# Four block quads for three in each feed-forward chunk, two of their weight sums taken from a DRAM scratch

## The reference

```
h = rms_norm(x, g_mix);   x = x + hybrid_mixer(h, ..., w_in, ..., w_out)
h = rms_norm(x, g_xattn); x = x + memory_cross_attention(h, rms_norm(mem, g_mem), w_xq, w_xkv, w_xo)
h = rms_norm(x, g_ffn)
x = x + (silu(h @ w_gate) * (h @ w_up)) @ w_down
return rms_norm(x, g_final)
```

## Time and profile before

| | |
|---|---|
| median of 3 runs | 1197.07 us (1196.96 to 1198.46) |
| the profiled execution | 1196.37 us, span 1194.8 us |
| TensorE clock granted | 0.998 |
| busy: PE, DVE, ACT, POOL | 99%, 78%, 56%, 7% |
| moved by DMA | 234.52 MB, 196 GB/s over the span |

### The profile page before, as it was taken

One profiled execution on the slowest core, in us unless ns is written; L12 is line 12 of the kernel. 1 busy time (PEld: TensorE's weight loads), 2 busy tenths in 40 slices (PEclk: granted clock), 3 DMA queues, 4 the chain that ended last, 5 costly groups with the idle time before them and its releaser, 6 DMA issues.

```text
span 1194.8 us, 16408 instructions
## 1 busy us (share of the span) xinstructions
PE 1184.5 (99%) x5418; PEld 983.0 (82%) x5418; DVE 934.2 (78%) x1176; ACT 674.8 (56%) x883; POOL 83.6 (7%) x89
## 2 busy tenths in 40 slices
PE   9999999999999999999999999999999999999997
PEld 8888888888888888888888888888888888888885
DVE  6655555557855666999899899989989889988886
ACT  5665554546644575765556555655555555555553
POOL 0042332200210000000000000000000000000000
PEclk9999999999999999999999999999999999999999
DMA  9865455556455544466566566566656656665663
GB/s 344 293 211 176 161 173 180 171 175 227 163 191 183 189 159 141 160 211 190 198 201 203 176 209 226 166 203 197 211 184 202 209 210 203 211 222 175 203 205 141
DMA packets 65851, 234.52 MB, mean 196 GB/s; under 512 B 7696, under 2 KB 8464, under 8 KB 65424
## 3 DMA queue, kind: packets, MB, share of 16 engines
q1 hardware_dynamic: 63072, 225.60, 57.2%
q10 hardware_dynamic: 2736, 8.35, 1.9%
HBM read 231.83 MB, written 2.10 MB: 196 GB/s over the span
## 4 chain that ended last, share of the span: by engine, by line
PE 90%; DVE 6%; DMA 2%; ACT 1%; issue 1%; POOLq 0%; POOL 0%; ACTq 0%; SPq 0%; DVEq 0%
PE ps L489 23%; PE ps L491 23%; PE ps L490 23%; PE ps L732 6%; PE ps L733 6%; PE ps L734 6%; DVE wlo L1624 3%; DMA raw<-w_stream 2%; PE ps L521 1%; DVE wsum L1631 1%; DVE raw L1619 0%; DVE raw L1627 0%; ACT whi L1145 0%; DMA par<-params 0%; PE ps L604 0%
## 5 line engine op out<-in xcount | busy, mean ns | idle before, releaser
L1145 ACT ACTIVATE whi<-raw 128x1024 fp32r<-128x1024 f32 (+1 forms) x310 | 303.9, 991 | 212.5 <-DMA raw<-w_stream 95.7
L1624 DVE TENSOR_TENSOR wlo<-raw,whi 128x1024 fp32r<-128x1024 f32 (+1 forms) x310 | 346.4, 1138 | 19.4 <-ACT whi L1145 18.8
L1270 DVE TENSOR_TENSOR wlo<-raw,whi 128x1024 fp32r<-128x1024 f32 x160 | 198.5, 1245 | 111.4 <-ACT whi L893 111.2
L489 PE MATMUL ps<-whi,ahi 128*128 128x512 f32 x600 | 235.9, 393 | 0.0
L491 PE MATMUL ps<-whi,alo 128*128 128x512 f32 x600 | 234.0, 390 | 0.0
L490 PE MATMUL ps<-wlo,ahi 128*128 128x512 f32 x600 | 233.7, 390 | 0.0
L893 ACT ACTIVATE whi<-raw 128x1024 fp32r<-128x1024 f32 x160 | 168.4, 1058 | 107.0 <-PE ps L491 96.3
L489 PE MATMUL ps<-whi,bhi 128*128 128x512 f32 x448 | 180.2, 402 | 0.5 <-DVE blo L1363 0.5
L491 PE MATMUL ps<-whi,blo 128*128 128x512 f32 x448 | 175.3, 391 | 0.0
L490 PE MATMUL ps<-wlo,bhi 128*128 128x512 f32 x448 | 174.7, 390 | 0.0
L491 PEld LDWEIGHTS ps<-whi,alo 128*128 128x128 f32 x600 | 112.7, 188 | 23.5
(11 more groups left out here) (244 smaller groups left out, 1498.9 us busy)
## 6 DMA issues: line engine op xcount, KB each, us to landing
raw<-w_stream SPq DMA_DIRECT2D x422, 512.0 KB, 4.2
res<-x_in ACTq DMA_DIRECT2D x4, 512.0 KB, 7.7
stage<-mem_in ACTq DMA_DIRECT2D x4, 512.0 KB, 6.5
proj<-mem_T ACTq DMA_DIRECT2D x2, 1024.0 KB, 7.7
stage<-x_T SPq DMA_DIRECT2D x7, 256.0 KB, 6.8
y_out<-res SPq DMA_DIRECT2D x4, 320.0 KB, 3.1
raw<-w_stream SPq DMA_DIRECT2D x4, 256.0 KB, 4.8
gfin<-g_final ACTq DMA_DIRECT2D x1, 1024.0 KB, 4.9
```

The source lines that it names most:

```text
L489: nc.tensor.matmul(bank, lhsT=a_h, rhs=w_h, start=start, stop=False)
L1145: nc.scalar.activation(whi_here, src, ACT.Copy).then_inc(hi_ready, 1)
L1270: vec.tensor_tensor(tile_pair(wlo, j), tile_pair(raw, j), tile_pair(whi, j).bitcast(f32), ALU.subtract).then_inc(lo_ready, 1)
L1624: vec.tensor_tensor(lo_here, src, hi_here.bitcast(f32), ALU.subtract).then_inc(lo_ready, 1)
```

## The change

1. **Quads.** `QUADS` goes from 3 to 4, at places 2, 7, 12 and 17 of a chunk that now has 24 places. One ordinary step stands between two quads; the others stand at 0, 1 and 21 to 23. Chunk 0 thus has two ordinary steps ahead of its first quad, not three, and the first is of K pair 4, not 3. A chunk has 8 ordinary steps, not 10. The parts have 6, 3, 6 and 6 matmuls.
2. **Weights of a quad.** The signs of the form are changed so that the sums are T = [B11 + B12, B22 + B12] and two more of 512 columns. The first tile of a quad is Z = [B11, B22] (512 KB), the second only B21 (H, 256 KB), and T (512 KB) is a third load, from the DRAM scratch `tsums`. DVE per quad: low parts of 1024, 512, 1024 and 1024 columns, and two sums of 512 (`wsum`). Before: low parts of 512, 1024, 1024 and 1024, and sums of 512, 512 and 1024. ACT per quad: 1024, 512, 1024 and 1024 columns; before: 512 and three times 1024.
3. **The scratch.** There are 44 T tiles. For each, SP copies Z to `tsums` (512 KB, DRAM to DRAM), one copy after every four loads from step 12 on, and the last 7 one after each of chunks 0 to 6. POOL then issues an accumulating transfer that adds B12 to both halves (`add_weights`); each waits for its copy and for the accumulation before it. They stand between POOL's other work: one before the head loop, two per head, one every third step from the convolution on, four between the last two roots, then a loop.
4. **Where T lies.** Chunk 0's T tiles go to free SBUF; from chunk 1 on they take the place of `res`. In chunk 0, after the seventh weight load, SP writes `res` (2 MB) to `res_kept`; in the down projection it loads it back in four pieces of 512 KB, at places 4, 8, 12 and 16 of `DOWN`, and `down_combine` waits for all four.
5. **Small ones.** `s_forms`, `s_lows` and the casts between them cover four quads; ACT makes two more copies of activations (`araw`); `P1_AT`, `COMBINED`, `SILU_AT` go from 17, 18, 21 to 19, 21, 23.

```diff
-QUADS = 3
+QUADS = 4
-QUAD_AT = (3, 9, 14)
+QUAD_AT = (2, 7, 12, 17)
-GATE_STEPS = {0: 3, 1: 4, 2: 5, 7: 6, 8: 7}
-UP_STEPS = {13: 3, 18: 4, 19: 5, 20: 6, 21: 7}
+GATE_STEPS = {0: 4, 1: 5, 6: 6, 11: 7}
+UP_STEPS = {16: 4, 21: 5, 22: 6, 23: 7}
+RAW_TILES = ("D0", "D1", "Z0", "H0", "D2", "Z1", "H1", "D3", "Z2", "H2", "D4", "Z3", "H3", "D5", "D6", "D7")
+T_LOAD_AT = {0: 0, 4: 1, 7: 2, 10: 3}
+RES_SAVE_AT, RES_BACK_AT = 6, (4, 8, 12, 16)
...
+                    if n in T_LOAD_AT:
+                        m = T_LOAD_AT[n]
+                        if m == 0:
+                            sp.wait_ge(t_summed, ci * (16 * QUADS) + 16 * QUADS * (c + 1))
+                        sp.dma_start(t_tile(c, m), tsums[ci * QUADS + (c * QUADS + m)]).then_inc(t_loaded[m], 16)
...
+                    if c == 0 and n == RES_SAVE_AT:
+                        await_out(sp, G_FF - 1)
+                        sp.dma_start(res_kept, res[:]).then_inc(res_saved, 16)
...
+                sp.dma_start(tsums[i - COPY_FROM], stream[i + (J_Z - COPY_FROM)]).then_inc(t_copied, 16)
...
+            def add_weights(m, first=False):
+
+                pool.wait_ge(t_copied, m * 16 + 16)
+                if not first:
+                    pool.wait_ge(t_summed, m * 16)
+                both = tsums[m].rearrange("p (h n) -> p h n", h=2)
+                b12 = stream[m + J_W][:, GC:KS * GC].unsqueeze(1).to_broadcast([P, 2, GC])
+                nc.gpsimd.dma_start(both, b12, accum_op=ALU.add).then_inc(t_summed, 16)
...
+                if part == 1:
+                    b22, b21 = tile_pair(raw, j)[:, GC:KS * GC], tile_pair(raw, j + 1)[:, 0:GC]
+                    dve.wait_ge(t_loaded[q % QUADS], ci * 16 + 16 * (q // QUADS + 1))
...
+                    vec.tensor_tensor(wsum[:, 0:GC], t_tile(q // QUADS, q % QUADS)[:, 0:GC], b22,
+                                      ALU.add).then_inc(w_sums, 1)
+                    dve.wait_ge(w_sums, ci * (2 * QUADS) + (2 * q + 1))
+                    vec.tensor_tensor(wsum[:, GC:KS * GC], wsum[:, 0:GC], b21, ALU.add).then_inc(w_sums, 1)
```

More of the change, by code:

```diff
@@ L464, in _ @@
                     rope(h + 2, n)
+                    for m in range(2):
+                        add_weights(i * 4 + (2 * n + m + 1))
             head_root(NH - 2)
             head_root(NH - 1)
+            m = 2 * (NH - 2) + 1
             for j in range((G_X + 1) * SPG, G_XQ * SPG):
```

191 lines of the change are left out of this document (143 added, 48 removed).

## The result

The changed kernel takes **1204.12 us** (median of 5 runs, 1202.66 to 1205.19), the one before 1197.08 (1196.96 to 1198.46) beside it: a ratio of 1.0055, with a 95% interval of 1.0041 to 1.007. It is 7 us slower, where 1193.9 was forecast, and outside the range of 1189.5 to 1201.5. The profiled execution took 1205.19 us, with a span of 1203.6.

What follows compares the result with a forecast made beforehand. PE's matmul work was taken to set the time. Terms of -7.5, +2.2, +0.3 and +1.8 summed to -3.2 us, from 1196.4 to 1193.2 against the profiled execution, a median of 1193.9 us; range 1189.5 to 1201.5.

Steps and rivals of the forecast that it cites:

- Fewer matmuls: Chunks: 180 matmuls each instead of 183, 33 fewer over eleven chunks at 0.227 us, -7.5 us.
- DVE and ACT in a running chunk: Running chunks: DVE falls from 30.3 to 29.8 us per chunk, `combine` covered with about 1 us left; no cost.
- Weight loads in a running chunk: Running chunks: SP's loads at 245 GB/s land in time, H having 7.4 us against 4.2 us; no cost.
- The third rival: Beside chunks 1 to 7, accumulations delay H to 8 or 9 us: 1197 to 1203 us in all, chance 0.18.
- Copies and accumulations in the first 160 steps: Beside the heads: 259 to 346 GB/s against 343 seen, ring leaves a load some 8 us; no cost.
- The start of chunk 0: Chunk 0: larger form sums and one more `araw` pair make DVE late and PE wait, +2.2 us, bounds 0 and 5.
- Saving the residual: Chunk 0: the 6.1 us write of `res` queues ahead of weight loads, next tile late, +0.3 us, bounds 0 and 6.
- The residual's return: Down projection: the piece at place 8 delays a load on the chain and lengthens PE's wait, +1.8 us, bounds 0 and 4.
- POOL held by its own transfers: Convolution: accumulations landing later than 14 us after issue delay POOL's roots and PE, 1204 us in all, chance 0.12.

Runs made afterwards that it cites:

- the fastest version: Changed kernel with late copies beside steps 52 to 79, accumulations spread over chunks, `up` before Z0's split, residual back in chunk 10, `gfin` at place 18: 1193.93 us (0.9965).

## Why the prediction was wrong

- **Fewer matmuls (-7.5): right.** Undisturbed chunks take 41.70 to 41.74 us where 41.72 was forecast; in the fastest version ten of them do.
- **DVE and ACT in a running chunk (nothing): right in the undisturbed chunks**, `combine` within three steps included. But about 1 us of slack was taken as enough at the boundary, and no row was read there for what stands ahead of `up`, which is the split of Z0.
- **Weight loads in a running chunk (nothing): this step failed.** Its allowance was worked out for H in a steady quad, 7.4 us, and set against a mean rate and a landing of 4.2 us. It did not ask when in the chunk an accumulation goes out. The third rival did name it, with H delayed "to 8 or 9 us"; measured were 8.0 to 9.2. That mechanism was right for a steady quad. At the boundary, where nearly all was paid, the load that counts is Z0 (6.9 to 7.8 us instead of at most 5.4), ahead of `up`, and no allowance was worked out for it. The rival's price (1 us in three to seven chunks, 3 to 9 in all) was nearly right too: chunks 2 to 5 paid 4.9 us over 41.7, and chunk 1 3.5. What was wrong is the sentence against it, "H must be in flight just then", with the chance of 0.18 that came of it. The copy's landing releases the accumulation and the copy stands at a fixed place in SP's order, so from the third boundary on it goes out within 1 us of Z0 each time, and not by chance.
- **Chunk 1** had no term, and it measured 3.5 us too long. Five accumulations back to back from 520.89 to 557.62 follow from `root(3)`, which POOL waits for from 456.19 to 519.84. The kernel before has that root too, so the burst could have been foreseen.
- **Copies and accumulations in the first 160 steps (nothing): right.** At most 0.3 us, in ring slots that leave 8 us.
- **The start of chunk 0 (+2.2): right in kind, short by 0.7.** Without any transfer the first transposes come 2.9 us later than before (540.13, 537.24). The waits are 1.47, 1.20 and 0.80 us where 1.3, 1.1 and 0.5 (with 0.15 more) were given. PE in order of time:

```profile
489.07 0.39 PE L588 MATMUL ps<-whi,oxlo 128*128 128x512 f32 x1
490.77 0.47 PE L586 MATMUL ps<-whi,ahi 128*128 128x512 f32 x1 [1.32 <-issue]
...
499.82 0.40 PE L831 MATMUL ps<-whi,alo 128*128 128x512 f32 x1
501.25 0.50 PE L829 MATMUL ps<-whi,sfh 128*128 128x512 f32 x1 [1.04 <-DVE alo L1396]
...
510.72 0.39 PE L831 MATMUL ps<-whi,alo 128*128 128x512 f32 x1
511.75 0.47 PE L586 MATMUL ps<-whi,ahi 128*128 128x512 f32 x1 [0.65 <-DVE wlo L1738]
```

- **Saving the residual (+0.3): not to be seen by itself.** It landed after 7.9 us where 6.1 was worked out, but the third wait of chunk 0 is the same 0.81 us without it. It mattered only together with accumulations beside it (3.24 us).
- **The residual's return (+1.8): right in kind, too large by about a third.** The part behind the last transposes is 2.1 us longer than before. Over all traces the return is worth about 1.2 us, with 1.4 to 2.3 us of PE waits near the pieces of places 8 and 12 against 0.3 to 0.9 without them there. The rest was not in the sum: even with the return elsewhere the part takes 234.8 us or more, 1.2 over before, and PE waits there for DVE's splits (0.63 and 0.75 us in the fastest version, near 1015 and 1052). What makes DVE later than before there was not tried and stays open.
- **POOL held by its own transfers: did not happen as priced.** An accumulation lands after 8.8 us (median of 44), within the 4.2 to 11.9 of the bounds and under the 14 that decide. The Trainium skill (DMA: Bandwidth & Descriptors, Anatomy of one DMA) gives the estimate of 3.2 us for it; the measurement is nearly three times that, and decides. Small waits of PE for a convolution's root do appear (0.24 us in the changed kernel, up to 0.89 in the fastest version).

Put together, the forecast of 1193.9 comes near the change without its transfers, 1194.72, in part because terms that were too small and too large cancel. The transfers cost 9.4 us more, and by the profiled spans (1203.6 and 1192.4) 2.2 us of the 11.2 between these two fall ahead of the first transposes, 8.0 in chunks 1 to 5 and 1.0 behind the last. Most of the 2.2 is a wait of 1.88 us for `up` at 542.32, behind a Z0 that took 7.1 us to land beside the first accumulation and the first late copy. The 1.0 is within what this part scatters.

## What to carry to other kernels

When a change adds a background transfer to a loop, a mean rate says little. Find out what releases the transfer, which fixes when it goes out in the loop, and which loads are issued in the 2 us behind it; those came 2 to 4 us late here. Then look at what stands ahead of the critical instruction in its engine's fixed order, because a late load is paid there. Giving the transfer a wait of its own that puts it behind the tight loads, or moving it into a stage with deep buffers, can be worth most of its cost without a byte less: here the two together gave back 6.9 of 9.4 us.
